# Grouping the GLA output products of a head pair by the tiling they use on TensorE

## The chip, the cores and the metric

The kernel runs on one core of a Trainium2 chip. The metric is device time in microseconds (us), the median of several runs. A core has TensorE (PE in the profile: matrix products; PEld is its weight load), VectorE (DVE), ScalarE (ACT), GpSimd (POOL) and SyncE (SP), which here only issues DMAs. Each engine takes its instructions in program order and meets the others through semaphores.

## The reference

The program computes two layers of a streaming encoder for two groups that share all weights: a prompt of 512 tokens and a sample of 32 tokens. Layer 1 mixes with gated linear attention (GLA) beside an mLSTM. What the change touches is the output `o` of GLA, in chunks of 64 tokens:

```python
def step(S, inp):                       # once per chunk of L = 64 tokens
    qc, kc, vc, lac = inp
    cum = jnp.cumsum(lac, axis=1)
    last = cum[:, -1:]
    ref = 0.5 * last
    att = jnp.einsum('blhd,bshd->bhls', qc * jnp.exp(cum - ref), kc * jnp.exp(ref - cum))
    att = jnp.where(causal, att, 0.0)
    o = (jnp.einsum('bhls,bshe->blhe', att, vc)
         + jnp.einsum('blhd,bhde->blhe', qc * jnp.exp(cum), S))
    S = jnp.exp(last[:, 0])[..., None] * S + jnp.einsum('bshd,bshe->bhde', kc * jnp.exp(last - cum), vc)
    return S, o
```

There are 4 heads with key width 64 and value width 128. Each output row is a sum of two products: attention times values inside the chunk, and queries times the state `S` from before the chunk. The prompt starts with `S = 0`, so its first chunk has no state product; the sample starts from a given state.

## The kernel before, in words

Everything is held transposed, features on the 128 partitions and tokens along the free axis. Nearly all work is the projections: an output tile of 128 features by 544 tokens is the product of 8 weight blocks with the activations, computed in split precision (weights and activations each as a high and a low part; lines 564 and 572 of the helpers, 48 matmuls per tile). TensorE's program is one list written by hand. In `gla_pe` the small products of GLA stand between these projections, `item(n)`, so that the other engines can work while TensorE projects.

GLA runs in two passes, pair 0 and pair 1, each over two heads `j` = 0, 1, which lie on partitions 0 to 63 and 64 to 127 of `Q3` (decayed queries) and `SG8` (the states after chunks 0 to 6). The 512 prompt tokens are four blocks of 128 (two chunks each). For each pair, `gla_scores_pe` makes the scores, `gla_kv_pe` the products that feed the states (line 1228 for the prompt, 1232 for the sample), VectorE makes the states from them (`gla_states_dve`, lines 1762 to 1769), and `gla_out_pe` makes the output. Head 0's output goes to the PSUM tensor `core_k` (`K`), head 1's to `core_j` (`J`); index 0 of the second axis is a bank of 512 columns for the prompt, index 1 a bank of which 128 columns take the sample.

In `gla_out_pe` a head's products stand block by block: for block 0 two products of 64 output rows (line 1248, 128 rows of contraction), for the others one product of 128 by 128 (line 1245); behind each the state products of its chunks, 64 by 64, with the output in the lower or upper 64 partitions (line 1251); last the sample's two products (1253 and 1254). The last product raises the semaphore `s_got` ("gla_out").

Who waits for `s_got`: VectorE takes the moments of the output (`gla_moments_dve`, line 1792), then the split of the next weight's low part (line 442), then the reciprocal deviation and the normalised output (line 1809). SyncE waits for it before it loads the next sample state (line 1082), and after pair 1 before `ml_states(0)` (lines 1098 and 1100), behind which stand two more weight loads (line 450). Weights come into two buffers in turn: SyncE loads (450), ScalarE makes the high part (437), VectorE the low part (442), TensorE uses both.

After pair 1 `item(13)` follows, and then the mLSTM's first head: `query_or_key` (1367), `values` (1360), which waits for the semaphore that line 1809 raises.

Of the kernel before, what the change touches and what calls it, by code (L numbers as in the profile page):

```python
# [28 lines left out]
P = 128  # L29
D = 1024  # L30
KD = D // P
TP, TS = 512, 32
T = TP + TS
# [9 lines left out]
NB = TP // P  # L43
# [116 lines left out]
def encoder(nc, t, out):  # L160

    with ExitStack() as ctx:
# [65 lines left out]
        def area(*shape):  # L228
            n = int(np.prod(shape))
            a = AREA[:, mark[0]:mark[0] + n]  # L230
            mark[0] += n
            assert mark[0] <= AREA_ALL, mark[0]
            return a.rearrange("p (a b) -> p a b", a=shape[0]) if len(shape) == 2 else a
# [29 lines left out]
        Q1, Q3 = area(T), area(T)  # L263
# [4 lines left out]
        VTG = [area(NB + 1, P), area(NB + 1, P)]  # L268
        AG = [area(NB + 1, P), area(NB + 1, P)]
        sums = mark[0]  # L270
        SG8 = area(8, P)
        SGN, SGF, SG0 = area(P), area(P), area(P)
# [57 lines left out]
        K = ctx.enter_context(nc.psum_tensor("core_k", [P, 2, 512], F32))  # L330
        J = ctx.enter_context(nc.psum_tensor("core_j", [P, 2, 512], F32))
# [903 lines left out]
        def gla_out_pe(pe, i):  # L1235

            pe.wait_ge(s_gst, i + 1)
            pe.wait_ge(s_gs0, 16 * i + 16)
            for j in range(2):
                q = slice(64 * j, 64 * j + 64)  # L1240
                dst = (K, J)[j]
                for b in range(NB):
                    cols = slice(b * P, (b + 1) * P)
                    if b:
                        pe.matmul(dst[:, 0, cols], AG[j][:, b, :], VTG[j][:, b, :], start=True, stop=False)
                    else:
                        for r in (slice(0, 64), slice(64, P)):
                            pe.matmul(dst[r, 0, cols], AG[j][:, b, r], VTG[j][:, b, :], start=True, stop=(r.start == 0))
                    for c in (2 * b, 2 * b + 1):
                        if c:  # L1250
                            pe.matmul(dst[64 * (c % 2):64 * (c % 2) + 64, 0, cols], Q3[q, 64 * c:64 * c + 64],
                                      SG8[q, c - 1, :], start=False, stop=True)
                pe.matmul(dst[0:TS, 1, 0:P], AG[j][0:TS, NB, 0:TS], VTG[j][0:TS, NB, :], start=True, stop=False)
                mm = pe.matmul(dst[0:TS, 1, 0:P], Q3[q, TP:T], SG0[q], start=False, stop=True)
            mm.then_inc(s_got, 1)

        def gla_turn_pe(pe, i, j):
# [25 lines left out]
        def gla_pe(pe):  # L1283
# [17 lines left out]
            gla_kv_pe(pe, 0)  # L1301
            item(6)
            gla_out_pe(pe, 0)
            for n in (7, 8):
                item(n)
# [17 lines left out]
            gla_kv_pe(pe, 1)  # L1323
            item(12)
            gla_out_pe(pe, 1)
            item(13)

# [1233 lines left out]
```

## Time and profile before

| | |
|---|---|
| time, median of 3 runs | 1445.29 us (1443.51 to 1447.14) |
| the profiled execution's own time | 1451.51 us |
| its span, first to last instruction | 1449.9 us |
| mean granted TensorE clock in it | 0.98 |
| TensorE busy | 1387.5 us (96%) |
| VectorE busy | 702.3 us (48%) |
| ScalarE busy | 473.9 us (33%) |
| `gla_out_pe`, pair 0, first product to the next projection | 9.57 us (802.33 to 811.90) |
| `gla_out_pe`, pair 1 | 7.49 us (858.67 to 866.16) |

Every time below is counted from the span's start. The busy time of PE counts overlapping matmuls once, and a matmul's recorded length is modelled and longer than the distance to the next one; so the distance between the starts of neighbouring matmuls is what counts. A product of 32-bit floats leaves two records in the trace ("x2" is one product). A form such as `64*64 64x128` is the tiling, rows*columns of the array that the product uses, and then the moving operand, partitions x elements.

### The profile page before, as it was taken

What the parts mean: (1) busy time and instruction counts of PE and PEld (TensorE: products, weight loads), DVE (VectorE), ACT (ScalarE), POOL (GpSimd) and SP (SyncE); (2) the same over time, 40 slices, a digit from 0 to 9 for tenths busy, and PEclk for the clock granted to TensorE, in tenths of its full rate; (3) what the DMA queues carried; (4) which work ended last, traced back from release to release, by engine and by line L of the source; (5) the groups of instructions that cost most, each with busy time, mean ns of one, the idle gap of its engine ahead of it and who ended that gap; (6) DMA issues with size and microseconds to landing.
All of it is one profiled execution on the core that took longest, in us unless ns stands there. A gap on an engine that the chain in (4) does not pass through costs nothing.

```text
span 1449.9 us, 28525 instructions
## 1 busy us (share of the span) xinstructions
PE 1387.5 (96%) x11025; PEld 1316.5 (91%) x11025; DVE 702.3 (48%) x1269; ACT 473.9 (33%) x728; POOL 83.9 (6%) x99
## 2 busy tenths in 40 slices
PE   5999999989999999999989998989899999999997
PEld 3888888879999999999969887879799999999997
DVE  4655655655333333333576456765633333333344
ACT  4354454433222222222355223323422222222233
POOL 0000000000110011001000000000011001100100
PEclk9899999999999999999999898999999999999998
DMA  9445444577244332222222213325122323332322
GB/s 351 142 142 151 145 123 152 193 241 246 87 138 137 88 87 87 87 87 80 69 61 74 78 29 85 77 70 195 50 87 87 100 75 87 87 100 75 87 78 85
DMA packets 224520, 163.12 MB, mean 113 GB/s; under 512 B 9346, under 2 KB 209732, under 8 KB 224332
## 3 DMA queue, kind: packets, MB, share of 16 engines
q1 hardware_dynamic: 212864, 119.42, 28.4%
q10 hardware_dynamic: 6764, 25.30, 4.6%
q0 software_dynamic: 4832, 17.58, 3.8%
q8 instruction: 41, 0.67, 0.2%
q14 instruction: 19, 0.16, 0.0%
HBM read 158.68 MB, written 3.59 MB: 112 GB/s over the span
## 4 chain that ended last, share of the span: by engine, by line
PE 87%; DVE 4%; DMA 3%; issue 2%; ACT 2%; ACTq 1%; DVEq 0%; SPq 0%
PE ring L564 48%; PE ring L572 23%; PE ring L605 5%; DMA weight_raw<-in_a_w_out 2%; PE core_j L480 1%; DVE normed_low L705 1%; DMA mixer_area<-in_w_mod 1%; ACTq L2279 1%; PE core_j L1360 0%; PE core_j L1391 0%; PE ring L1367 0%; DMA mixer_area<-in_state_mlstm_n 0%; DMA out_y_p<-mixer_area 0%; PE core_j L1406 0%; DMA weight_raw<-in_c_w_in 0%
## 5 line engine op out<-in xcount | busy, mean ns | idle before, releaser
L564 PE MATMUL ring<-normed_high,weight_high 128*128 128x272 f32 x2016 | 423.7, 291 | 0.0
L564 PE MATMUL ring<-normed_low,weight_high 128*128 128x272 f32 x2016 | 419.1, 289 | 0.0
L442 DVE TENSOR_TENSOR weight_low<-weight_raw,weight_high 128x1024 fp32r<-128x1024 f32 x197 | 261.9, 1330 | 143.3 <-ACT weight_high L437 142.0
L564 PEld LDWEIGHTS ring<-normed_high,weight_high 128*128 128x128 f32 x2016 | 316.9, 189 | 6.2 <-issue 5.4
L564 PEld LDWEIGHTS ring<-normed_low,weight_high 128*128 128x128 f32 x2016 | 316.6, 189 | 0.0
L437 ACT ACTIVATE weight_high<-weight_raw 128x1024 fp32r<-128x1024 f32 x197 | 207.0, 1051 | 226.0 <-PE ring L605 149.0
L572 PE MATMUL ring<-normed_high,weight_low 128*128 128x272 f32 x2016 | 273.4, 288 | 0.0
L572 PEld LDWEIGHTS ring<-normed_high,weight_low 128*128 128x128 f32 x2016 | 260.8, 188 | 0.0
L564 PE MATMUL ring<-mixed_high,weight_high 128*128 128x272 f32 x824 | 173.1, 291 | 5.2 <-ACT weight_high L437 3.5
L564 PE MATMUL ring<-mixed_low,weight_high 128*128 128x272 f32 x824 | 171.8, 290 | 0.0
L564 PEld LDWEIGHTS ring<-mixed_high,weight_high 128*128 128x128 f32 x824 | 130.6, 191 | 6.7 <-issue 6.5
L715 DVE SCALAR_TENSOR_TENSOR residual<-ring,modulation,residual 128x272 f32 (+3 forms) x192 | 66.1, 400 | 142.0 <-PE ring L605 141.8
L564 PEld LDWEIGHTS ring<-mixed_low,weight_high 128*128 128x128 f32 x824 | 130.2, 190 | 0.0
L572 PE MATMUL ring<-mixed_high,weight_low 128*128 128x272 f32 x824 | 113.3, 288 | 0.0
L952 POOL TENSOR_TENSOR mixed_low<-norm_temp,mixed_high 128x544 f32 x44 | 60.2, 1369 | 824.9 <-ACT mixed_high L894 824.9
L572 PEld LDWEIGHTS ring<-mixed_high,weight_low 128*128 128x128 f32 x824 | 107.1, 188 | 0.2 <-issue 0.2
L894 ACT ACTIVATE mixed_high<-norm_temp 128x544 f32 (+1 forms) x44 | 29.0, 658 | 226.8 <-DVE norm_temp L1034 226.8
L1034 DVE SCALAR_TENSOR_TENSOR norm_temp<-norm_value,ring 128x544 f32<-128x544 f32 x44 | 31.7, 720 | 134.5 <-PE ring L572 134.5
L1028 DVE SCALAR_TENSOR_TENSOR norm_value<-norm_temp,ring 128x544 f32<-128x544 f32 x44 | 31.7, 721 | 110.1 <-ACT norm_temp L891 110.1
L891 ACT ACTIVATE norm_temp<-ring 128x544 f32<-128x544 f32 x44 | 27.4, 624 | 153.6 <-PE ring L572 151.4
L631 ACT ACTIVATE norm_temp<-residual 128x544 f32 (+1 forms) x40 | 26.3, 657 | 76.1 <-DVE residual L715 75.6
L641 DVE TENSOR_TENSOR norm_rstd<-norm_rstd,norm_temp 128x544 f32<-128x544 f32 x40 | 29.0, 724 | 36.4 <-ACT norm_temp L631 36.4
(419 smaller groups left out, 1219.2 us busy)
## 6 DMA issues: line engine op xcount, KB each, us to landing
weight_raw<-in_w_ffn_in SPq DMA_DIRECT2D x88, 512.0 KB, 3.9
mixer_area<-in_w_mod ACTq DMA_DIRECT2D x12, 2048.0 KB, 11.5
mod_weight<-in_w_mod POOLq DMA_DIRECT2D x16, 1024.0 KB, 5.9
weight_raw<-in_w_ffn_out SPq DMA_DIRECT2D x32, 512.0 KB, 4.1
weight_raw<-in_a_w_in SPq DMA_DIRECT2D x24, 512.0 KB, 6.1
weight_raw<-in_c_w_in SPq DMA_DIRECT2D x20, 512.0 KB, 3.9
mixer_area<-in_w_mod SPq DMA_DIRECT2D x7, 1024.0 KB, 13.3
weight_raw<-in_w_ffn_out SPq DMA_DIRECT2D x16, 384.0 KB, 3.3
```

What stands on the lines that cost most here:

```text
L437: act.activation(WH[n.slot][:], RAW[n.slot][:], ACT.Copy).then_inc(s_hi, 1)
L442: dve.tensor_tensor(WL[n.slot][:], RAW[n.slot][:], WH[n.slot][:].bitcast(F32), ALU.subtract).then_inc(s_lo, 1)
L564: pe.matmul(PS[p.slot][:, half, 0:HALF], WH[n.slot][:, k, :], x[:, k, half * HALF:(half + 1) * HALF], start=(k == 0 and x is moving[0]), s ...
L572: last = pe.matmul(PS[p.slot][:, half, 0:HALF], WL[n.slot][:, k, :], moving[0][:, k, half * HALF:(half + 1) * HALF], start=False, stop=(k ...
L605: last = pe.matmul(PS[p.slot][:, half, 0:HALF], w[n.slot][:, k, :], x[:, k, half * HALF:(half + 1) * HALF], start=(k == 0 and w is WH and ...
L641: dve.tensor_tensor(NR[:, :], NR[:, :], TMP[:, j, :], ALU.add).then_inc(s_add, 1)
L715: ins = dve.scalar_tensor_tensor(out=X[:, m, lo:hi], in0=PS[p.slot][:, half, a:a + hi - lo], scalar=MOD[:, gate + m, g:g + 1], in1=X[:, m, ...
L891: act.activation(pair(TMP[:, 0, :]), ring(Turn(p, 0, 2, i)), ACT.Tanh, scale=0.5).then_inc(s_fth, 1)
L894: act.activation(GH[:, i, :], TMP[:, 1, :], ACT.Copy).then_inc(s_gah, 1)
L952: pool.tensor_tensor(GL[:, i, :], TMP[:, 1, :], GH[:, i, :].bitcast(F32), ALU.subtract).then_inc(s_glf, 1)
L1028: dve.scalar_tensor_tensor(out=pair(NV), in0=pair(TMP[:, 0, :]), scalar=1.0, in1=ring(gi), op0=ALU.add, op1=ALU.mult).then_inc(s_free[gi.s ...
L1034: dve.scalar_tensor_tensor(out=pair(TMP[:, 1, :]), in0=pair(NV), scalar=0.5, in1=ring(ui), op0=ALU.mult, op1=ALU.mult).then_inc(s_free[ui. ...
```

## The change

The products of both heads of a pair are issued in three groups. First come the 14 state products, for chunks 1 to 7, the two heads in turn; then the sample's two state products and its two attention products; then the eight 128x128 block products, which now accumulate onto what the state products left. The two half products of block 0 are one 128x128 product like the others. So 26 products stand in place of 28 for each pair. No wait and no other engine's instruction is changed; `s_got` is again raised by the last product.

```diff
             pe.wait_ge(s_gst, i + 1)
             pe.wait_ge(s_gs0, 16 * i + 16)
+            for c in range(1, 2 * NB):
+                for j in range(2):
+                    q = slice(64 * j, 64 * j + 64)
+                    pe.matmul((K, J)[j][64 * (c % 2):64 * (c % 2) + 64, 0, c // 2 * P:(c // 2 + 1) * P],
+                              Q3[q, 64 * c:64 * c + 64], SG8[q, c - 1, :], start=(c <= 2), stop=(c >= 2 * NB - 2),
+                              skip_group_check=True)
             for j in range(2):
                 q = slice(64 * j, 64 * j + 64)
-                dst = (K, J)[j]
+                pe.matmul((K, J)[j][0:TS, 1, 0:P], Q3[q, TP:T], SG0[q], start=True, stop=False)
+            for j in range(2):
+                pe.matmul((K, J)[j][0:TS, 1, 0:P], AG[j][0:TS, NB, 0:TS], VTG[j][0:TS, NB, :], start=False, stop=True)
+            for j in range(2):
                 for b in range(NB):
-                    cols = slice(b * P, (b + 1) * P)
-                    if b:
-                        pe.matmul(dst[:, 0, cols], AG[j][:, b, :], VTG[j][:, b, :], start=True, stop=False)
-                    else:
-                        for r in (slice(0, 64), slice(64, P)):
-                            pe.matmul(dst[r, 0, cols], AG[j][:, b, r], VTG[j][:, b, :], start=True, stop=(r.start == 0))
-                    for c in (2 * b, 2 * b + 1):
-                        if c:
-                            pe.matmul(dst[64 * (c % 2):64 * (c % 2) + 64, 0, cols], Q3[q, 64 * c:64 * c + 64],
-                                      SG8[q, c - 1, :], start=False, stop=True)
-                pe.matmul(dst[0:TS, 1, 0:P], AG[j][0:TS, NB, 0:TS], VTG[j][0:TS, NB, :], start=True, stop=False)
-                mm = pe.matmul(dst[0:TS, 1, 0:P], Q3[q, TP:T], SG0[q], start=False, stop=True)
+                    mm = pe.matmul((K, J)[j][:, 0, b * P:(b + 1) * P], AG[j][:, b, :], VTG[j][:, b, :],
+                                   start=False, stop=True, skip_group_check=True)
             mm.then_inc(s_got, 1)
```

On TensorE, at pair 0's output, this stood before (`core_k` is head 0's output, `core_j` head 1's; the operands all lie in `mixer_area`; the size is that of the moving operand, and "x2" here is two products):

```order
L572 MATMUL ring<-normed_high,weight_low 128x272 x16
L1248 MATMUL core_k<-mixer_area 64x128 x2
L1251 MATMUL core_k<-mixer_area 64x128
L1245 MATMUL core_k<-mixer_area 128x128
L1251 MATMUL core_k<-mixer_area 64x128 x2
...
L1253 MATMUL core_k<-mixer_area 32x128
L1254 MATMUL core_k<-mixer_area 32x128
L1248 MATMUL core_j<-mixer_area 64x128 x2
```

The same place now, with the state products at line 1242, the sample's at 1247 and 1249, the blocks at 1252:

```order
L572 MATMUL ring<-normed_high,weight_low 128x272 x16
L1242 MATMUL core_k<-mixer_area 64x128
L1242 MATMUL core_j<-mixer_area 64x128
...
L1247 MATMUL core_k<-mixer_area 32x128
L1247 MATMUL core_j<-mixer_area 32x128
L1249 MATMUL core_k<-mixer_area 32x128
L1249 MATMUL core_j<-mixer_area 32x128
L1252 MATMUL core_k<-mixer_area 128x128 x4
L1252 MATMUL core_j<-mixer_area 128x128 x4
```

Where blocks and state products alternated within one head, the state products of both heads now stand together (seven such couples) and the eight blocks stand together at the end.

The end of pair 1's output on TensorE, with the first matmuls of `item(13)`, before:

```order
L1245 MATMUL core_j<-mixer_area 128x128
L1251 MATMUL core_j<-mixer_area 64x128 x2
L1253 MATMUL core_j<-mixer_area 32x128
L1254 MATMUL core_j<-mixer_area 32x128
L564 MATMUL ring<-normed_high,weight_high 128x272 x2
```

and now:

```order
L1249 MATMUL core_k<-mixer_area 32x128
L1249 MATMUL core_j<-mixer_area 32x128
L1252 MATMUL core_k<-mixer_area 128x128 x4
L1252 MATMUL core_j<-mixer_area 128x128 x4
L564 MATMUL ring<-normed_high,weight_high 128x272 x2
```

The product that raises `s_got` is now a 128x128 block of head 1 instead of the sample's state product; what stands in front of the output and behind it is the same.

## Rows read from the trace of the kernel before

**Rows 1.** Page: span, then busy time and share of the engines.

```profile
span 1449.9 us, 28525 instructions
PE 1387.5 (96%) x11025; PEld 1316.5 (91%) x11025; DVE 702.3 (48%) x1269; ACT 473.9 (33%) x728; POOL 83.9 (6%) x99
```

**Rows 2.** Page: the chain that ended last, by engine.

```profile
PE 87%; DVE 4%; DMA 3%; issue 2%; ACT 2%; ACTq 1%; DVEq 0%; SPq 0%
```

**Rows 3.** Timeline of PE, pair 1's output: start, length, line, form, records.

```profile
858.67 0.44 PE L1248 MATMUL core_k<-mixer_area 128*64 128x128 f32 x4
859.04 0.43 PE L1251 MATMUL core_k<-mixer_area 64*64 64x128 f32 x2
859.40 0.49 PE L1245 MATMUL core_k<-mixer_area 128*128 128x128 f32 x2
859.82 0.44 PE L1251 MATMUL core_k<-mixer_area 64*64 64x128 f32 x4
860.18 0.49 PE L1245 MATMUL core_k<-mixer_area 128*128 128x128 f32 x2
...
861.75 0.40 PE L1253 MATMUL core_k<-mixer_area 32*32 32x128 f32 x2
862.08 0.40 PE L1254 MATMUL core_k<-mixer_area 64*32 64x128 f32 x2
862.41 0.44 PE L1248 MATMUL core_j<-mixer_area 128*64 128x128 f32 x4
...
866.16 0.52 PE L564 MATMUL ring<-normed_high,weight_high 128*128 128x272 f32 x2
```

**Rows 4.** Timeline of PE, the 16 products of line 1228, pair 0.

```profile
794.71 0.33 PE L1228 MATMUL core_k<-mixer_area 64*64 64x128 f32 x2
794.72 0.33 PE L1228 MATMUL core_j<-mixer_area 64*64 64x128 f32 x2
794.87 0.28 PE L1228 MATMUL core_k<-mixer_area 64*64 64x128 f32 x2
794.88 0.28 PE L1228 MATMUL core_j<-mixer_area 64*64 64x128 f32 x2
794.98 0.28 PE L1228 MATMUL core_k<-mixer_area 64*64 64x128 f32 x2
...
795.75 0.43 PE L1232 MATMUL core_k<-mixer_area 32*64 32x128 f32 x4
```

**Rows 5.** Timeline of PE, 128*128 products in a row (mLSTM).

```profile
897.57 0.39 PE L1417 MATMUL core_k<-mixer_area 128*128 128x129 f32 x2
897.79 0.39 PE L1415 MATMUL core_k<-mixer_area 128*128 128x129 f32 x2
```

**Rows 6.** Windows: stretch, length, busy per engine (x instructions), granted clock, DMA.

```profile
802.33:806.90 4.57, 4.57 (x36) 2.61 (x35) 0.00 (x0) 1.57 (x2) 0.00 (x0) 1.00 0.37 107
806.90:811.90 5.00, 5.00 (x22) 2.57 (x22) 0.00 (x0) 0.00 (x0) 0.00 (x0) 0.50 0.00 0
811.90:820.35 8.45, 8.45 (x50) 8.45 (x50) 7.68 (x39) 0.00 (x0) 0.00 (x0) 0.69 0.47 129
858.67:866.16 7.49, 7.49 (x58) 4.26 (x57) 0.95 (x3) 0.62 (x1) 0.00 (x0) 1.00 0.01 2
866.16:872.29 6.13, 6.13 (x49) 6.13 (x49) 2.07 (x10) 0.00 (x0) 0.11 (x1) 1.00 0.71 182
```

**Rows 7.** Timeline of ACT and DVE behind pair 0: idle before and its releaser.

```profile
820.61 1.06 ACT L437 ACTIVATE weight_high<-weight_raw 128x1024 fp32r<-128x1024 f32 x1 [16.60 <-PE ring L572]
826.63 0.72 DVE L1776 TENSOR_TENSOR mixer_area<-ring,mixer_area 128x544 f32<-128x544 f32 x1 [3.29 <-PE ring L572]
```

**Rows 8.** Chain of waits behind pair 1's output, then PE's timeline there.

```profile
866.26 0.47 SPq L1098
867.48 5.23 DMA weight_raw<-in_c_w_in
878.62 1.36 DVE mixer_area L1809 x4
```

```profile
880.02 2.64 PE L1360 MATMUL core_j<-mod_weight,mixer_area 128*128 128x128 f32 x10 [3.77 <-DVE mixer_area L1809]
```

## The prediction

> **What bounds the kernel now.** I read the page first. TensorE is busy for 1387.5 us of a span of 1449.9 [rows 1], and the chain that ended last lies on it for 87% [rows 2]: what TensorE saves in a place where it waits for nobody comes off the end, unless it waits longer further on. Next I read TensorE's timeline at `gla_out_pe`. At pair 1 the stretch from the first output product to the next projection is 7.49 us, with TensorE busy all through at clock 1.00, 2.4 GHz [rows 3, 6]. The distances between starts tell why so few products take so long. One state product of tiling 64*64 takes 0.36 us (859.04 to 859.40); two of them, for the two halves of the output partitions, also take 0.36 (859.82 to 860.18). A block of 128*128 takes 0.42 (859.40 to 859.82), the two half products of block 0 together 0.37, each sample product 0.33 (861.75, 862.08, 862.41) [rows 3]. Where the tiling doesn't change, a 128*128 product takes 0.22 (897.57 to 897.79), though it streams one column more [rows 5]. So a product is 0.22, and a change of tiling costs some 0.20 when it goes to 128*128, 0.14 to 64*64, and 0.11 to the sample's forms.
>
> Third, the rows of line 1228: 16 products of 64*64 without a change of tiling. Records for both row halves (`core_k` takes products of the upper 64 rows, `core_j` of the lower) start within 0.01 us of each other, two in each bank; the next such four come at 794.87 and 794.98, so four records each 0.11 us. The 16 products take 1.04 us in all (794.71 to 795.75) [rows 4]: four tiles work at once.
>
> **The change part by part, at full clock.** Before: per head 0.37 + 0.36 + 3 x 0.42 + 3 x 0.36 + 2 x 0.33 = 3.73, for two heads 7.46; the trace has 7.49 for both [rows 3, 6].
>
> State products: 14 of 64*64 in a run. Neighbours differ in the row half (head 0 reads partitions 0 to 63 and writes `core_k`, head 1 reads 64 to 127 and writes `core_j`), and every four of them use four different tiles, as at line 1228. 28 records by four are 7 steps of 0.11 = 0.77, and the rest of line 1228's stretch (1.04 - 8 x 0.11 = 0.16) is its change of tiling: 0.93. No run with this order of tiles is in the trace. From below, 0.77; from above, one product after the other at 0.22 each, 3.08 + 0.14 = 3.22. I take 0.93, since line 1228 differs from it only in the order within four.
>
> Sample, state: two products on different row halves and banks, one after a change of tiling: 0.33 if they overlap, 0.66 if not. I take 0.33.
>
> Sample, attention: both heads read partitions 0 to 31 and write the same 32, so they use one tile in turn: 0.33 + 0.22 = 0.55; between 0.33 and 0.66.
>
> Blocks: eight 128*128 in a row, one change of tiling in front: 8 x 0.22 + 0.20 = 1.96. From below 1.76, without the change; from above 8 x 0.42 = 3.36, as now. That they accumulate on what the state products left costs nothing by rows 5, where line 1417 adds to what 1415 wrote at the same 0.22.
>
> Sum: 0.93 + 0.33 + 0.55 + 1.96 = 3.77 against 7.49, so 3.72 less for each pair and 7.44 for both. The two products that fall away (block 0's halves become one block) are in this sum.
>
> **The clock at pair 0.** In the profiled execution pair 0's output took 4.57 + 5.00 = 9.57 us, because the granted clock fell to 0.50 (1.2 GHz) at about 806.9, while TensorE was changing its tiling at almost every product; it stayed there into the next projection, which took 8.45 us against 6.13 for the same projection behind pair 1 [rows 6]. That is 2.08 + 2.32 = 4.40 us. Pair 1 ran the same products without a fall. With the change, the stretch of small products is under 2 us, and dense 128*128 work follows; I expect this fall to go wherever it occurs. It need not occur in each execution: the profiled one is 1451.51 against the median 1445.29, 6.2 more. I count half of it, 2.2.
>
> **What lies behind it.** Behind pair 0 the others wait for TensorE, not it for them: ScalarE sat idle 16.60 us before the next high part, until a projection on TensorE ended, and VectorE 3.29 [rows 7]. Weight loads and moments are started by `s_got` or by these two, so they move up too. Behind pair 1 TensorE does wait, 3.77 us before line 1360, for VectorE's line 1809 [rows 8]. But the chain to it begins at the output's end: SyncE issues line 1098 at 866.26, 0.10 after the next projection began, then the weight whose transfer takes 5.23, then the splits on ScalarE and VectorE, then 1809. All of it moves up with the output, so the wait stays 3.77 and the gain isn't eaten. No wait is added, no DMA is moved in any queue.
>
> Against the profiled execution's own time: 1451.51 - 7.44 - 4.40 = 1439.7. Against the median: 1445.29 - 7.44 - 2.2 = 1435.65, rounded to **1436 us**.
>
> **Rivals.**
> 1. *Only two tiles at once.* Each product leaves two records. If these stand next to each other, the second must wait 0.11 for the first on the same tile, and if starts keep program order, everything behind waits too: one product each 0.11, so 14 x 0.11 + 0.16 = 1.70 instead of 0.93, 1.5 us for both pairs: 1437.2. Rows 4 speak against it: four records start within 0.02 there, though that order puts the two column halves first and the new one the row halves. The Trainium skill has such a rule, "TensorE: Matmul & The Clock Gate", Part 3 (What overlaps and what doesn't): matmuls start and end strictly in program order. By it alone the sum would be this rival's; line 1228's rows don't show such a limit.
> 2. *The wait behind pair 1 eats its gain.* If line 1809 or the weight load were held by something older than the output, TensorE would wait 3.72 longer, and 1439.4 results. For it: TensorE is idle just there. Against it: the chain from 866.26 to 880.02 has no link that starts earlier [rows 8].
> 3. *The clock falls elsewhere.* Nothing is won from pair 0's clock, and one more stretch at 0.50 comes at the same price, 4.40, for instance at the 3.77 us of idleness before line 1360: 1445.29 - 7.44 + 4.40 = 1442.3, within 0.3%. For it: the same code had a fall in pair 0 and none in pair 1 [rows 6]. Against it: the change takes slow small work away and adds no gap.
> 4. *Slower: alternating row halves make each state product pay what a change of tiling pays.* Each would then take the 0.36 of a lone one: 14 x 0.36 = 5.04, with samples 4 x 0.33 and blocks 8 x 0.42 = 3.36 (if accumulation on two other tiles' results drains as well): 9.72, 2.23 more for each pair, so 1445.29 + 4.5 = 1449.8. With the other parts as in my sum (0.33 + 0.55 + 1.96 = 2.84) it decides for slower from (7.49 - 2.84) / 14 = 0.33 for a state product. Against it: two products on different column halves took no more than one [rows 3], and line 1228 changes the row half every two products at 0.11 per four records [rows 4].
>
> That the order isn't what the diff says is ruled out by the instructions shown above.
>
> **How the numbers follow.** Forecast 0.74, rival 1 0.08, rival 2 0.06, rival 3 0.09, rival 4 0.03. The likeliest is 1436. Its own range comes from the share of the clock's fall (none: 1437.9; all: 1433.5) and the bounds of the parts (0.77 + 0.33 + 0.33 + 1.76 = 3.19, so 1.2 less for both pairs; the dearer sample 0.66 + 0.66 gives 0.9 more), and the runs of before differ by 1.8 from their median: 1432 to 1439.5. Rivals 1 and 2 end at or inside it or just beyond, so 1432 to 1441 holds eight in ten; rivals 3 and 4 are left out with the edges. About 0.3% (4.3 us) is what a measurement of this kernel can tell from no change. Faster by more: most of the forecast, rivals 1 and 2 and a little of rival 3, 0.85. Within: rival 3 and the near edge of the others, 0.11. Slower: rival 4 and chance falls of the clock, 0.04.
>
> **What would show it right or wrong.** In the profile of the changed kernel: line 1242 takes about 0.93 us from its first start to line 1247's; 1247 0.33; 1249 0.55; 1252 about 1.96 to the next L564; the whole 3.8 for each pair at clock 1.00. If 1242 takes 1.7, rival 1 holds; 5, rival 4. The clock stays at 1.00 from 802 to 815. TensorE's idle time before line 1360 stays near 3.77; if it is 7.5, rival 2 holds. I am wrong as a whole if these stretches shrink as said and the median doesn't fall by 6 us.

## The result and the profile after

The changed kernel takes 1438.38 us (median of 9 runs, 1435.19 to 1442.09); the kernel before took 1447.03 us beside it (9 runs, 1443.51 to 1449.04). The ratio is 0.9947 with a 95% interval of 0.9934 to 0.9959: the medians differ by 8.65 us, the ratio stands for 7.7 and its interval for 5.9 to 9.6. The forecast was 1436 us, 1432 to 1441. The profiled execution took 1441.51 us, span 1439.9, against 1451.51 and 1449.9 before.

The page of the changed kernel, its span, the busy time and share of each engine, and the chain that ended last by engine ("issue" is time in which an engine waited for nothing that the profile shows, a q stands for an engine's sequencer):

```profile
span 1439.9 us, 28509 instructions
PE 1378.0 (96%) x11017; PEld 1313.0 (91%) x11017; DVE 702.4 (49%) x1269; ACT 474.0 (33%) x728; POOL 84.1 (6%) x99
...
PE 86%; DVE 5%; DMA 4%; issue 2%; ACT 2%; ACTq 1%; SPq 0%; DVEq 0%
```

TensorE's busy time fell by 9.5 us (1387.5 to 1378.0) and the span by 10.0, while the other engines' busy times moved by 0.2 at most [rows 1]. Nothing else was made cheaper, and nothing else became the bound.

The windows of the changed kernel: stretch, its length, busy time of PE, PEld, DVE, ACT and POOL (x instructions), granted clock, DMA share and GB/s. The stretches are pair 0's output, the projection behind it, pair 1's output, the projection behind that:

```profile
803.45:807.17 3.72, 3.72 (x53) 3.14 (x53) 0.00 (x0) 1.57 (x2) 0.00 (x0) 1.00 0.44 127
807.17:813.30 6.13, 6.13 (x52) 6.13 (x51) 5.51 (x31) 0.00 (x0) 0.00 (x0) 1.00 0.27 70
851.66:855.38 3.72, 3.72 (x53) 3.14 (x53) 0.96 (x3) 0.62 (x1) 0.00 (x0) 1.00 0.02 4
855.38:861.50 6.12, 6.12 (x51) 6.12 (x50) 2.07 (x10) 0.00 (x0) 0.11 (x1) 1.00 0.71 179
```

Set against [rows 6], each output stretch is 3.72 us where pair 1's was 7.49, and the clock is 1.00, 2.4 GHz, through both stretches and both projections. Along the program: TensorE reaches pair 0 1.12 us later than before (803.45 against 802.33), which comes from an earlier place, and the end of the next projection 7.05 earlier (813.30 against 820.35), 8.17 won, of which 5.85 in the output (9.57 to 3.72) and 2.32 in the projection. At pair 1's end it is 10.78 ahead (855.38 against 866.16), and 10.0 at the end of the span. The two outputs and the projection behind pair 0 thus gave 11.94, close to the 7.44 + 4.40 = 11.84 that was forecast against this execution; the 1439.7 worked out from it was missed by 1.8 (1441.51), 1.12 of it lost ahead of pair 0 and 0.8 behind pair 1, where nothing was changed.

TensorE's timeline of the changed kernel at pair 0's output: start, length, line, form, records. The first four rows are the first records of four products:

```profile
803.45 0.32 PE L1242 MATMUL core_k<-mixer_area 64*64 64x128 f32 x1
803.46 0.32 PE L1242 MATMUL core_j<-mixer_area 64*64 64x128 f32 x1
803.47 0.32 PE L1242 MATMUL core_k<-mixer_area 64*64 64x128 f32 x1
803.47 0.32 PE L1242 MATMUL core_j<-mixer_area 64*64 64x128 f32 x1
...
804.16 0.27 PE L1242 MATMUL core_k<-mixer_area 64*64 64x128 f32 x1
804.16 0.27 PE L1242 MATMUL core_j<-mixer_area 64*64 64x128 f32 x1
804.27 0.27 PE L1242 MATMUL core_k<-mixer_area 64*64 64x128 f32 x1
804.27 0.27 PE L1242 MATMUL core_j<-mixer_area 64*64 64x128 f32 x1
804.47 0.29 PE L1247 MATMUL core_k<-mixer_area 64*32 64x128 f32 x1
...
804.81 0.40 PE L1249 MATMUL core_k<-mixer_area 32*32 32x128 f32 x2
...
805.36 1.16 PE L1252 MATMUL core_k<-mixer_area 128*128 128x128 f32 x8
806.36 1.06 PE L1252 MATMUL core_j<-mixer_area 128*128 128x128 f32 x8
807.17 0.50 PE L564 MATMUL ring<-normed_high,weight_high 128*128 128x272 f32 x2
807.50 0.41 PE L564 MATMUL ring<-normed_low,weight_high 128*128 128x272 f32 x2
807.75 0.41 PE L564 MATMUL ring<-normed_high,weight_high 128*128 128x272 f32 x2
```

The states take 1.02 us (803.45 to 804.47), the sample's states 0.34, its attention 0.55, the eight blocks 1.81: 3.72. Four records start within 0.02 us, as in [rows 4]; the last two steps, at 804.16 and 804.27, hold only two.

The chain behind pair 1's output in the changed kernel (start, length, what), and TensorE's wait before the mLSTM's values, which answer to [rows 8] (1809 is line 1808 now, 1360 is 1359):

```profile
855.66 0.47 SPq L1098
...
856.88 4.97 DMA weight_raw<-in_c_w_in
```

```profile
869.16 2.64 PE L1359 MATMUL core_j<-mod_weight,mixer_area 128*128 128x128 f32 x10 [3.77 <-DVE mixer_area L1808]
```

The chain begins 10.6 us earlier (855.66 against 866.26) and ends 10.9 earlier (869.16 against 880.02), and the wait at its end is 3.77 us as before.

### The profile page after: what moved, and what is told of

Same layout as the page of the kernel before. It is cut to its first block, busy times and chain, and to the rows that moved or that the text cites. A ratio compares the mean times of both kernels' runs of the same rounds, so it can differ in the third digit from the quotient of the medians.

```text
span 1439.9 us, 28509 instructions
## 1 busy us (share of the span) xinstructions
PE 1378.0 (96%) x11017; PEld 1313.0 (91%) x11017; DVE 702.4 (49%) x1269; ACT 474.0 (33%) x728; POOL 84.1 (6%) x99
## 4 chain that ended last, share of the span: by engine, by line
PE 86%; DVE 5%; DMA 4%; issue 2%; ACT 2%; ACTq 1%; SPq 0%; DVEq 0%
PE ring L564 47%; PE ring L572 23%; PE ring L605 5%; DMA weight_raw<-in_a_w_out 2%; PE core_j L480 1%; DVE normed_low L705 1%; DMA weight_raw<-in_w_ffn_in 1%; DMA mixer_area<-in_w_mod 1%; ACTq L2278 1%; PE core_j L1359 0%; PE core_j L1390 0%; ACT weight_high L437 0%; DVE weight_low L442 0%; PE ring L1366 0%; DMA out_y_p<-mixer_area 0%
```

## The experiments

Times of the first four stand beside the kernel before at 1447.97 us (30 runs), those of the next four beside it at 1447.78 (17 runs). The diffs are against the changed kernel, that of experiment 5 against the kernel before; "..." and comments stand for code left out.

**1. Grouped at pair 0 alone, and 2. at pair 1 alone.**

```diff
-            for c in range(1, 2 * NB):
+            if i == 0:                      # 2: if i == 1
+                # the grouped products
...
+            else:
+                # the products in the old order
```

> The new order at pair 0's output alone; pair 1 as before. Theory (the gain is what each output stretch loses at full clock, 3.7 us each): pair 0's stretch 3.72 us, pair 1's 7.49, TensorE's idle time before the mLSTM's values 3.77 as in both kernels; 3.8 us less than before, about 1443.2. Rival (the fall of the granted clock at pair 0 is a regular part of the gain): 2.2 us more, about 1441.0, and clearly less than with pair 1 alone.

> The new order at pair 1's output alone; pair 0 as before. Theory: pair 1's stretch 3.72 us, and the whole of 3.8 us comes off the end, 1443.2, since the chain behind it begins with its last product; pair 0's stretch 7.49, if the clock holds. Rival (the wait before the mLSTM's values eats it): TensorE's idle time there grows from 3.77 to 7.5 us and the time stays at 1447. In this profile pair 0's old order is seen once more: a fall of the clock at about 807 us, or none, tells how regular that fall is.

Measured: pair 0 alone 1442.29 us, ratio 0.9971 [0.9958, 0.9984], 5.7 less; pair 1 alone 1443.72, ratio 0.9982 [0.9964, 0.9999], 4.3 less. The windows with pair 0 alone grouped: its output, then pair 1's in the old order in two pieces, then the projection behind that.

```profile
802.05:805.77 3.72, 3.72 (x53) 3.14 (x53) 0.00 (x0) 1.57 (x2) 0.00 (x0) 1.00 0.45 128
...
850.27:854.10 3.83, 3.83 (x31) 2.21 (x32) 0.95 (x3) 0.62 (x1) 0.00 (x0) 1.00 0.00 0
854.10:860.35 6.25, 6.25 (x28) 3.16 (x28) 0.00 (x0) 0.00 (x0) 0.00 (x0) 0.50 0.01 3
860.35:868.25 7.90, 7.90 (x49) 7.90 (x49) 2.80 (x11) 1.70 (x3) 0.11 (x1) 0.75 0.65 176
```

The same with pair 1 alone grouped (pair 0's output in the old order, the projection behind it, pair 1's output), and then TensorE's wait in it:

```profile
802.92:810.41 7.49, 7.49 (x57) 4.26 (x56) 0.00 (x0) 1.57 (x2) 0.00 (x0) 1.00 0.23 66
810.41:818.09 7.68, 7.68 (x49) 7.68 (x49) 7.12 (x38) 0.00 (x0) 0.00 (x0) 0.78 0.47 129
856.45:860.17 3.72, 3.72 (x54) 3.14 (x53) 0.95 (x3) 0.62 (x1) 0.00 (x0) 1.00 0.02 4
```

```profile
873.71 2.64 PE L1377 MATMUL core_j<-mod_weight,mixer_area 128*128 128x128 f32 x10 [3.77 <-DVE mixer_area L1826]
```

Each pair wins by itself, and 5.7 + 4.3 = 10.0 agrees with the whole's 8.65 within the intervals. These are wide (2.3 to 6.1 us for pair 0, 0.1 to 5.2 for pair 1): both hold the 3.8 of the theory, and pair 0 alone, between its two times on record (1443.2 and 1441.0), doesn't settle what the clock is worth. Pair 1 alone leaves the wait at 3.77, so its gain isn't eaten: rival 2 falls. With pair 0 alone grouped, the clock fell at pair 1, in the old order, as it had at pair 0 in the trace of before; pair 0, grouped, had no fall. With pair 1 alone grouped it fell right behind pair 0's old order, for a shorter time.

**3. Heads one after the other.** The same state products, all of head 0 and then all of head 1.

```diff
-            for c in range(1, 2 * NB):
-                for j in range(2):
+            for j in range(2):
+                for c in range(1, 2 * NB):
```

> The same groups by tiling, but the seven state products of head 0 first and then those of head 1. Theory (neighbours on four different tiles run together): here neighbours share the row half, two tiles at a time; four products on one tile are 4 x 0.22 = 0.88 us per head, so 1.8 to 1.9 us for the 14 instead of 1.02, a stretch of 4.55 instead of 3.72 and 1.7 us more than with the heads in turn in the whole kernel. Rival A (only the number of tiling changes counts, the order inside a group does not): 1.02 and 3.72 as with the heads in turn.

Measured: 1441.39 us, ratio 0.9962 [0.9946, 0.9978]; both stretches 4.20 us. TensorE's timeline of this kernel:

```profile
802.84 0.76 PE L1242 MATMUL core_k<-mixer_area 64*64 64x128 f32 x9
803.33 0.32 PE L1242 MATMUL core_j<-mixer_area 64*64 64x128 f32 x1
...
803.65 0.27 PE L1242 MATMUL core_k<-mixer_area 64*64 64x128 f32 x1
803.71 0.70 PE L1242 MATMUL core_j<-mixer_area 64*64 64x128 f32 x8
804.35 0.29 PE L1247 MATMUL core_k<-mixer_area 64*32 64x128 f32 x1
...
807.04 0.50 PE L564 MATMUL ring<-normed_high,weight_high 128*128 128x272 f32 x2
```

The states take 1.51 us: neither number that was on record. Head 1's first record starts at 803.33, while records of head 0, which stands ahead in the program, go on until 803.65. So starts do not keep program order across row halves, but the engine reaches only some products ahead; for the rest of the time one head's two tiles (both column halves of one row half) work and the other head's stand idle. The order that alternates heads is worth 0.48 us per pair.

**4. Two blocks, then their states.** The states still rotate over four tiles, but the tiling changes between every couple of blocks and its state products, eight times for the prompt instead of twice. The blocks come first here and the state products add to them.

```diff
+            for b in range(NB):
+                for j in range(2):
+                    pe.matmul((K, J)[j][:, 0, b * P:(b + 1) * P], AG[j][:, b, :], VTG[j][:, b, :], ...)
+                for c in (2 * b, 2 * b + 1):
+                    for j in range(2 if c else 0):
+                        ...
```

> The old sequence of block and state products, but with the heads in turn: two blocks, then the state products of that block for both heads (two for block 0, four for the others), four times, then the sample's products as in the change. Block 0 is one product here too. Tiling changes of the prompt's products: 8 instead of 2 in the change and 14 before. Theory (a product 0.22, a change 0.20 to 128*128 and 0.14 to 64*64, four tiles together): 4 x (0.44 + 0.20) + 4 x (0.22 + 0.14) + 0.34 + 0.55 = 4.9 us a pair, 5.2 us less than before in all, 1441.8. Rival A' (only the overlap of tiles counts, changes are free): 3.7 a pair as with the change. Rival B (overlap counts for nothing, each product pays for itself): 8 x 0.42 + 14 x 0.36 + 0.9 = 9.3 a pair, slower than before.

Measured: 1442.07 us, ratio 0.9953 [0.9934, 0.9972]; stretches 4.86 and 4.85. TensorE's timeline: the start at pair 0, one block of both heads, the start of the next, the end:

```profile
803.66 0.38 PE L1241 MATMUL core_k<-mixer_area 128*128 128x128 f32 x2
...
804.57 0.49 PE L1241 MATMUL core_k<-mixer_area 128*128 128x128 f32 x2
804.89 0.39 PE L1241 MATMUL core_j<-mixer_area 128*128 128x128 f32 x2
805.21 0.32 PE L1246 MATMUL core_k<-mixer_area 64*64 64x128 f32 x1
...
805.59 0.49 PE L1241 MATMUL core_k<-mixer_area 128*128 128x128 f32 x2
...
808.52 0.52 PE L564 MATMUL ring<-normed_high,weight_high 128*128 128x272 f32 x2
```

Two blocks take 0.64 (804.57 to 805.21), of which 0.44 is two products at 0.22 and 0.20 the changes of tiling around them; four state products take 0.38. The stretch came out where the price of a change, read from the trace of before, put it: about 4.9. The two rivals on record both fall: that changes of tiling are free (3.7), and that overlap counts for nothing and each product pays for itself (9.3).

**5. One block 0, nothing else.** The old order with block 0 as one product per head.

```diff
-                    if b:
-                        ...
-                    else:
-                        for r in (slice(0, 64), slice(64, P)):
-                            ...
+                    pe.matmul(dst[:, 0, cols], AG[j][:, b, :], VTG[j][:, b, :], start=True, stop=False, ...)
```

> The old order with one edit of the change alone: block 0's two half products become one 128x128 product. Theory: no change of tiling falls away for head 1 (the sample's form goes to 128*128 instead of 128*64), so each stretch is 7.49 less at most 0.15 us for head 0, 7.35 to 7.5, and the time that of before. Rival (the two products fewer are the gain): 0.44 less a pair. The old alternation of tilings is seen twice more in this profile: in two of the three executions profiled so far with it, three of four such stretches had a fall of the granted clock in them or right behind; if that comes from the alternation, one or two falls are to be expected between 800 and 880 us before the wait for line 1360's like, and with the grouped order none.

Measured: 1447.08 us, ratio 1.0001 [0.9988, 1.0015]. Windows, both outputs:

```profile
803.09:810.57 7.48, 7.48 (x54) 4.35 (x52) 0.00 (x0) 1.57 (x2) 0.00 (x0) 1.00 0.24 63
854.99:862.47 7.48, 7.48 (x55) 4.35 (x53) 1.04 (x3) 0.62 (x1) 0.00 (x0) 1.00 0.01 2
```

7.48 against 7.49: two products fewer per pair, without the grouping, are worth 0.01 us. The gain is the grouping's. The traces of before, 1 and 2 had shown one fall of the clock each, three in four stretches of the old order; the one or two that were expected here on that ground didn't come, in neither stretch nor behind it.

**6. Column halves first.** Four products use the same four tiles in another order.

```diff
-            for c in range(1, 2 * NB):
-                for j in range(2):
+            for j, c in [(j, c) for b in range(NB) for j in range(2) for c in (2 * b, 2 * b + 1) if c]:
+                if True:
```

> The changed kernel with the state products of each block in the order of line 1228: both column halves of head 0, then both of head 1. Theory (any four neighbours on four tiles run together): the same 1.02 us for the 14 products, a stretch of 3.72, and the time of the change. Rival (the order of halves matters: with two records of one product next to each other only two tiles run at once in one of the orders): 1.5 us or more.

Measured: 1439.88 us, ratio 0.9950 [0.9932, 0.9968]. The windows of both outputs:

```profile
801.37:805.09 3.72, 3.72 (x54) 3.14 (x53) 0.00 (x0) 1.57 (x2) 0.00 (x0) 1.00 0.45 133
849.58:853.30 3.72, 3.72 (x53) 3.14 (x53) 0.96 (x3) 0.62 (x1) 0.00 (x0) 1.00 0.02 4
```

The states take 1.02 in it (801.37 to 802.39), as in the changed kernel: within four the order is free.

**7. The sample's state as a 64*64 product.** It takes 64 output rows (32 of them zero queries, read by nobody) and stands in the lower tiles with the state products, so that these tiles too have four products each and one change of tiling goes. `Q3` is 32 columns longer for it, which GpSimd sets to zero once (not shown in the diff).

```diff
+            for j in range(2):
+                q = slice(64 * j, 64 * j + 64)
+                pe.matmul((K, J)[j][0:64, 1, 0:P], Q3[q, TP:TP + 64], SG0[q], start=True, stop=False, ...)
             for c in range(1, 2 * NB):
...
-                pe.matmul((K, J)[j][0:TS, 1, 0:P], Q3[q, TP:T], SG0[q], start=True, stop=False)
```

> The changed kernel, but the sample's two state products are made 64*64 as well (32 columns of zeros behind the queries fill the tile; the 32 more output rows are read by nobody) and stand first among the state products. GpSimd sets the zeros once. Theory: the two tiles of the lower column half have three products each in the change, the others four, so the two more fit into the same eight steps: 16 products in 1.02 us as at line 1228 (1.04), line 1247's 0.34 falls away, a stretch of 3.38 instead of 3.72, 0.7 us less in the kernel than the change, too little for the time to tell. Rival (each product adds its share): 16/14 of 1.02 = 1.17, a stretch of 3.55.

Measured: 1438.31 us, ratio 0.9941 [0.9926, 0.9956]; stretches 3.39. TensorE's timeline at pair 0 (line 1246 the prompt's state products, 1242 the sample's):

```profile
803.92 0.32 PE L1242 MATMUL core_k<-mixer_area 64*64 64x128 f32 x1
...
804.95 0.40 PE L1250 MATMUL core_k<-mixer_area 32*32 32x128 f32 x2
...
807.31 0.49 PE L564 MATMUL ring<-normed_high,weight_high 128*128 128x272 f32 x2
```

Sixteen products take 1.03 us (803.92 to 804.95), where fourteen took 1.02. So the fullest tile sets the length: chunks 1, 3, 5 and 7 all go to the upper column half (output partitions 64 to 127), four products of two records on one tile for each head, 8 steps of 0.11 and 0.16 around them. The sample's states became free, 0.33 less per pair.

**8. The changed kernel beside 5 to 7.**

> The changed kernel once more, beside the others of this set: 3.72 us a pair, no fall of the clock at the two stretches, 8 to 9 us less than before; with the two single pairs at 5.7 and 4.3 less, their sum 10.0 is expected within the interval of the whole.

Measured: 1438.96 us, ratio 0.9939 [0.9923, 0.9955]; 8.8 us less. Both stretches:

```profile
802.98:806.69 3.71, 3.71 (x53) 3.13 (x53) 0.00 (x0) 1.57 (x2) 0.00 (x0) 1.00 0.44 129
851.19:854.90 3.71, 3.71 (x53) 3.13 (x53) 0.95 (x3) 0.62 (x1) 0.00 (x0) 1.00 0.02 4
```

The result repeats in a second comparison. Experiment 7's 0.65 us on top of it (1438.31 against 1438.96) is what its stretches shrank by, but its interval and this one's lie over each other: as a whole time it is not shown.

**9 and 10. The kernel before, twice more, for the clock.** No edit.

> The kernel before once more, unchanged, for its profile: its two output stretches add to the six stretches in the old order seen so far, of which three had the granted clock fall to 1.2 GHz in them or within 1 us behind them. If changing the tiling at almost every product is what brings the fall there, about half of this run's and the next run's stretches show one. If falls begin just anywhere (eight in a span of 1450 us), one begins in a given stretch of 8.5 us in 5 of 100 cases: none here. Where the clock holds, each stretch takes 7.49 us.

> The same kernel and the same question as the run ahead of it: about two of the four stretches of these two runs with a fall if the alternation brings it, none if falls begin just anywhere.

Measured: 1446.17 and 1448.25 us, one run each; a third run of it beside them took 1441.84. Windows of the first's two outputs, both at full clock:

```profile
804.78:812.27 7.49, 7.49 (x57) 4.26 (x57) 0.00 (x0) 1.57 (x2) 0.00 (x0) 1.00 0.22 63
856.72:864.21 7.49, 7.49 (x57) 4.25 (x56) 0.96 (x3) 0.62 (x1) 0.00 (x0) 1.00 0.01 2
```

and of the second's: pair 0 whole, pair 1 in two pieces.

```profile
804.84:812.34 7.50, 7.50 (x58) 4.26 (x57) 0.00 (x0) 1.57 (x2) 0.00 (x0) 1.00 0.22 61
...
856.79:860.54 3.75, 3.75 (x30) 2.13 (x29) 0.96 (x3) 0.62 (x1) 0.00 (x0) 0.99 0.00 0
860.54:866.94 6.40, 6.40 (x30) 3.31 (x29) 0.00 (x0) 0.00 (x0) 0.00 (x0) 0.50 0.01 3
```

One of four stretches: between the two expectations (two, and none), so it decides for neither. With those of before, 1, 2 and 5, the traces now show ten output stretches in the old order. In three of them the clock fell, each time about half way (4.57, 3.83 and 3.75 us after the start), and in one it fell 0.2 us behind the end. Of the fourteen stretches with grouped products or couples of blocks none shows a fall in it or within 1 us behind it. If all 24 had the same chance, the four would all lie among the ten in 2 of 100 cases. But three of the four are those that suggested the idea; the six stretches profiled since (5, 9, 10) show one. And the two kinds differ in length as well as in alternation: 7.5 us against 3.4 to 4.9. So the tally suggests that the old order brings the fall, in some executions; it doesn't show it, and no run was made that changes the alternation alone.

## Why the prediction was right, step by step

- **The bound.** TensorE waits for nobody at these places, and what it saves comes off the end: shown by experiments 1 and 2, where each pair alone makes the kernel faster, by times whose intervals hold the 3.77.
- **States, 0.93 predicted, 1.02 measured.** The step counted 28 records by four and got 7 steps. But a step needs four different tiles, and the upper column half has four products a head where the lower has three, so 8 steps are needed, two of them half empty, as many as line 1228's 16 products took. Experiment 7 shows it: two more products, in the lower tiles, cost nothing. The count of records was the wrong number; the fullest tile's was the right one.
- **Sample, 0.33 and 0.55 predicted, 0.34 and 0.55 measured.** The two state products on different row halves overlap; the two attention products on one tile stand one behind the other.
- **Blocks, 1.96 predicted, 1.81 measured.** Within the bounds 1.76 and 3.36. In the old order a block starts the next product 0.42 later [rows 3], while a couple in experiment 4 takes 0.64, so the price of 0.20 holds for a couple between state products. In the run of eight only 0.05 is left over 8 x 0.22, because the distance from the first block to the projection doesn't hold all of the price: at the far end the projection's first two starts are 0.33 apart (807.17, 807.50), in a running projection 0.25. So 0.08 us that the sum put on the blocks stands at the projection's start. Why it stands there, with no change of tiling in front of the projection, is open. It takes nothing off the gain: the projection behind pair 1 takes 6.12 where it took 6.13 [rows 6].
- **Sum, 3.77 predicted, 3.72 measured** per pair; the two errors, +0.09 and -0.15, nearly cancel, which is luck. For both pairs 7.54 less at full clock against 7.44.
- **The removed products are not the gain**: without the grouping they are worth 0.01 us per pair (experiment 5). No run puts them back into the grouped order.
- **The clock, 2.2 counted.** To count half of one fall was a choice between none and all of it, not a reading. In the profiled pair the fall of pair 0 went with its whole price: 8.17 won there, 3.77 by the products and 4.40 by the clock, as worked out. What it is worth in the median is less certain: 8.65 - 7.54 = 1.1 in the first comparison and 8.8 - 7.54 = 1.3 in the second, with intervals of -1.6 to 2.0 and -1.0 to 3.6; the first ends below 2.2. The four falls seen in ten stretches cost 4.40, 4.36, about 4.3 (10.15 and 7.80 us for the output and the projection behind it in run 10) and 1.55 (7.68 against 6.13), so on average 1.5 per stretch and 2.9 for a kernel with two. A third measure is the mean granted clock that each run lists: the share missing to 1, times the run's time, is 26.8 us on average in the 47 runs of the kernel before that stand beside the experiments and 24.9 in 15 of the changed one (experiment 8 with them), 1.9 less, with an interval of 0.6 to 3.3. That something is won from the clock is so borne out, and 2.2 lies within; as a price it is an estimate, since TensorE also waits in such stretches (busy for 8.88 of the 10.30 us from 878.60 in the trace of before), and experiment 3, grouped too, lists 26.7. The size stays open.
- **What lies behind.** The wait before the values is 3.77 us as before and 3.77 with pair 1 alone grouped: the weight load, the splits and line 1808 all hang on the output's end and moved up with it.
- **Rivals.** Rival 1 (only two tiles at once, 1.70 for the states) falls: four records start within 0.02 us and the states take 1.02. The Trainium skill's "TensorE: Matmul & The Clock Gate", Part 3 (What overlaps and what doesn't), lets matmuls start strictly in program order. The trace does not agree with that for these two-record products: in experiment 3 head 1 starts at 803.33 and head 0 still starts records at 803.65. Rival 2 falls by experiment 2. Rival 3: the changed kernel's trace has a fall at 742.3 (below) that the one of before lacks, but it lies 61 us ahead of the first changed product, so it isn't the fall of pair 0 put off; both traces have one near the wait before the values (868.6 and 878.6), so nothing shows that the fall of pair 0 moved there, and over all runs the clock's loss got smaller, not larger. Rival 4 falls: a state product takes 1.02 / 14 = 0.07, far from 0.36.

The window of that fall in the changed kernel (columns as above):

```profile
742.30:745.80 3.50, 3.50 (x14) 2.96 (x15) 3.50 (x9) 2.14 (x5) 0.04 (x1) 0.52 0.01 2
```

The medians leave 1438.38 - 1435.65 = 2.7 us: the kernel before was itself 1.7 slower in this comparison (1447.03) than in the three runs the forecast started from (1445.29), and the other 1.0 is the 1.1 that the medians leave for the clock in place of 2.2, less the 0.1 more won by the products. That 1.0 is within the noise.

## What to carry to other kernels

A small product on TensorE is priced by the change of tiling in front of it as much as by its columns: here 0.42 us for a block between others' tilings and 0.22 in a run. Group products by tiling, let neighbours use different tiles, and count the steps by the fullest tile, not by the number of products; a product that fitted an idle tile was free here (experiment 7). Read the prices in the trace from distances between starts, at places where the same tiling runs in a row and where it changes, and check that the engine's saving isn't given back at its next wait.

## What the runs showed of the hardware that was not expected

- Records of products on different row halves of the array start out of program order, but only some products ahead: with 14 products of one row half's tiles in two runs of seven, the second run began 0.49 us after the first, when nine of its 14 records had started and together with the tenth (experiment 3).
- Two products on the two column halves of one row half work at once: 0.11 us per two records there. All four tiles together also need 0.11 per four records.
- The clock fell to 1.2 GHz in or right behind four of ten stretches in the old order, which changed the tiling at almost every product, though the profile has TensorE busy throughout them, and in none of fourteen shorter ones that changed it less often. That changes of tiling bring the clock down is only what this tally suggests.
- A change of tiling has a price: 0.20 us to 128*128 and 0.14 to 64*64 at 2.4 GHz, as read from the trace of before and borne out by experiment 4. The Trainium skill's "TensorEngine Tiling (Array Packing)", Key Properties, says that a change of tiling mode drains the engine. The prices fit that; no run shows what the engine does in that time.
